# Attention steps ahead of the weight pieces in each turn, and a last slab that makes its two output tiles one behind the other

## The reference, cut to what matters

```python
x = x + _moba(rms(x), w_qkv, w_o)
x = x + conv_ffn(rms(x));  x = rms(x)
x = x + 0.5 * (1 + ga1) * swiglu(mod(rms(x)), w1_gate, w1_up, w1_down)
x = x + (1 + ga2) * hybrid_mixer(mod(rms(x)), w_in, ..., w_o)
x = x + 0.5 * (1 + ga3) * swiglu(mod(rms(x)), w2_gate, w2_up, w2_down)
```

## Time and profile before

| | |
|---|---|
| median of three runs | 819.49 us (819.26 to 819.83) |
| the profiled execution | 819.52 us |
| its span, first to last instruction | 817.3 us, 2.2 us less |
| TensorE busy | 802.3 us (98%) |
| VectorE busy | 644.4 us (79%) |
| ScalarE busy | 487.0 us (60%) |
| HBM read | 177.27 MB, 218 GB/s over the span |

### The profile page before, as it was taken

The page is one execution under the profiler, slowest core; times in us unless marked ns, Lnnn a source line. Parts: engine busy times, 40 slices in busy tenths (PEclk is TensorE's granted clock), DMA queues, the critical chain, the costliest instruction groups (busy, mean ns, idle before and its releaser), DMA issues.

```text
span 817.3 us, 16917 instructions
## 1 busy us (share of the span) xinstructions
PE 802.3 (98%) x6862; PEld 780.7 (96%) x6862; DVE 644.4 (79%) x1333; ACT 487.0 (60%) x1015; POOL 21.2 (3%) x53
## 2 busy tenths in 40 slices
PE   7999999999999999999999999899999999999998
PEld 7999998999999999999999999889889999999998
DVE  5788887888899887999988786977667896775551
ACT  6754566767767565756554556665655775555440
POOL 1000000000000000000000000700000000000000
PEclk9999999999999999999999999999999999999999
DMA  8777673765565998489998887545334578665540
GB/s 290 260 234 226 200 267 128 235 199 188 189 225 166 324 308 286 144 295 336 361 333 292 288 263 222 167 134 175 120 118 156 156 249 274 207 199 194 194 155 27
DMA packets 150013, 179.44 MB, mean 220 GB/s; under 512 B 5680, under 2 KB 139568, under 8 KB 149936
## 3 DMA queue, kind: packets, MB, share of 16 engines
q1 hardware_dynamic: 147680, 177.22, 65.8%
q10 hardware_dynamic: 1232, 1.11, 0.4%
q0 software_dynamic: 1024, 0.03, 0.1%
HBM read 177.27 MB, written 1.05 MB: 218 GB/s over the span
## 4 chain that ended last, share of the span: by engine, by line
PE 77%; DVE 4%; ACT 2%; issue 1%; DVEq 0%; ACTq 0%
PE bank L1349 24%; PE bank L1352 24%; PE bank L1353 24%; DVE wlo L970 1%; PE bank L1451 1%; PE bank L1439 1%; PE bank L1468 0%; PE bank L1370 0%; PE bank L1402 0%; DVE yb L1010 0%; PE bank L1418 0%; DVE A L1021 0%; ACT B L748 0%; PE bank L1395 0%; ACT sq L768 0%
## 5 line engine op out<-in xcount | busy, mean ns | idle before, releaser
L970 DVE TENSOR_TENSOR wlo<-raw,whi 128x512 fp32r<-128x512 f32 x528 | 342.7, 683 | 69.4 <-ACT whi L727 68.7
L727 ACT ACTIVATE whi<-raw 128x512 fp32r<-128x512 f32 x528 | 307.3, 622 | 97.1 <-PE bank L1353 85.2
L1349 PE MATMUL bank<-A,whi 128*128 128x256 f32 x1264 | 357.3, 283 | 3.4 <-DVE wlo L970 2.6
L1352 PE MATMUL bank<-A,whi 128*128 128x256 f32 x1264 | 350.6, 277 | 0.1
L1353 PE MATMUL bank<-A,wlo 128*128 128x256 f32 x1264 | 350.2, 277 | 0.0
L1349 PEld LDWEIGHTS bank<-A,whi 128*128 128x128 f32 x1264 | 237.7, 188 | 6.5 <-DVE wlo L970 3.5
L1352 PEld LDWEIGHTS bank<-A,whi 128*128 128x128 f32 x1264 | 237.7, 188 | 1.2 <-issue 1.0
L1353 PEld LDWEIGHTS bank<-A,wlo 128*128 128x128 f32 x1264 | 237.8, 188 | 0.0
L1349 PE MATMUL bank<-Hhi,whi 128*128 128x256 f32 x528 | 146.2, 277 | 0.0
L1353 PE MATMUL bank<-Hhi,wlo 128*128 128x256 f32 x528 | 145.9, 276 | 0.0
L1352 PE MATMUL bank<-Hlo,whi 128*128 128x256 f32 x528 | 145.9, 276 | 0.0
(11 more groups left out here) (150 smaller groups left out, 811.0 us busy)
## 6 DMA issues: line engine op xcount, KB each, us to landing
mring<-in_w_mod SPq DMA_DIRECT2D x72, 512.0 KB, 6.4
raw<-in_ffn_w_up SPq DMA_DIRECT2D x22, 1024.0 KB, 5.1
raw<-in_w_gate SPq DMA_DIRECT2D x22, 1024.0 KB, 5.7
raw<-in_w_up SPq DMA_DIRECT2D x22, 1024.0 KB, 6.0
raw<-in_w_down SPq DMA_DIRECT2D x16, 1024.0 KB, 5.4
raw<-in_w_in SPq DMA_DIRECT2D x12, 1024.0 KB, 5.4
raw<-in_moba_w_qkv SPq DMA_DIRECT2D x11, 1024.0 KB, 5.5
raw<-in_ffn_w_down SPq DMA_DIRECT2D x8, 1024.0 KB, 6.2
```

The source lines that it names most:

```text
L727: act.activation(whi[:, i % SPL, k0:k1, 0:width], raw[:, i % RAW, k0:k1, 0:width], ACT.Copy).then_inc(s_whi, 1)
L970: dve.tensor_tensor(lo, raw[:, i % RAW, k0:k1, 0:width], hi.bitcast(F32), ALU.subtract).then_inc(s_wlo, 1)
L1349: pe.matmul(o, hi, xh, start=kg == 0 and not (j and halved(g)), stop=False)
L1352: pe.matmul(o, hi, xl, start=False, stop=False)
```

## The change

In the main loop of the plan `attend()` stands ahead of `fill()`. So in each turn the steps of the attention come first in the queues of ScalarE and VectorE, and the hi and lo of later weights behind them. TensorE has no step in `fill`, SP none in `attend`. The transfers keep their order among themselves.

In the last slab TensorE makes tile 6 from all k-tiles as their pieces come, and at the last k-tile the whole of tile 7. A new semaphore, `s_ahead`, says that tile 6 is done; the eviction of tile 6 waits for it alone, that of tile 7 waits for the slab.

```diff
@@ main loop of the plan
                     offer(i + SPL, kt + 1)
+                    attend()
                     if i > 0:
                         fill(pieces(tag, c0, kt))
-                    attend()
@@ VectorE, evict
-                if part == 0 and g not in by_silu:
+                if g == len(groups) - 1:
+                    need.wait_ge(s_ahead, 1)
+                elif part == 0 and g not in by_silu:
                     need.wait_ge(s_chunk, chunk_of_group(g))
...
+                            if n == KD - 1:
+                                need.wait_ge(s_chunk, chunk_of_group(g))
@@ TensorE, multiply
+                if i == len(slabs) - 1:
+                    last_slab(i, kt)
+                    return
...
+            def last_slab(i, kt):
+                ph, tag, c0, k0, nk = slabs[i][:5]
+                g = plan.group_of[i]
+                for j, k in [(0, kt)] + [(1, k) for k in range(nk if kt == nk - 1 else 0)]:
+                    final = k == nk - 1
+                    xh, xl, ncol = here(tag, ph, k0 + k, g)
+                    hi = whi[:, i % SPL, k, j * P:j * P + P]
+                    lo = wlo[:, i % SPL, k, j * P:j * P + P]
+                    o = at(g, j, 0, ncol)
+                    pe.matmul(o, hi, xh, start=False, stop=False)
+                    pe.matmul(o, hi, xl, start=False, stop=False)
+                    ins = pe.matmul(o, lo, xh, start=False, stop=final)
+                    if j == 0 and final:
+                        ins.then_inc(s_ahead, 1)
+                    elif final or (j == 0 and k % 2 == 1):
+                        ins.then_inc(s_chunk, 1)
```

More of the change, by code:

```diff
@@ L503, in build_program @@
         s_xeven, s_xscaled = sem("s_xeven"), sem("s_xscaled")
+        s_ahead = sem("s_ahead")
         s_cond, s_cact, s_msum, s_mod = sem("s_cond"), sem("s_cact"), sem("s_msum"), sem("s_mod")
```

## The result

The changed kernel takes **827.13 us**, the median of 5 runs (825.02 to 830.85), against 819.49 before (5 runs, 819.06 to 819.83). The ratio is 1.0092, 95% interval 1.0076 to 1.0109: slower, by 7.6 us. The forecast was 825.2 us. The runs of the changed kernel lie further apart than those of the kernel before, and in these five the time goes with the mean granted clock of the run: 825.02 and 825.93 at 1.000, 827.13 and 827.49 at 0.998, 830.85 at 0.994. The profiled execution is that last one, the slowest, and this must be kept in mind with all its rows: its span is 828.6 us, 11.3 more than before.

The account below looks back on a forecast made before the run. TensorE, busy for 98% of the span, was taken to bound the kernel. Swap losses of 5.41 us in qkv1 and 0.66 at head 24, less 0.42 at the tail, gave 5.65 us and 825.2 us, range 823.5 to 827.0, wider 821.8 to 828.0.

Parts of the forecast that it names:

- The swap in qkv1: Heads 0, 4 and 8 each lose 1.28 us, head 12 loses 1.57; sum 5.41 us.
- the same lo and eviction come in: At head 0, one lo and one eviction delay scale as at head 4, costing 1.28 us.
- qkv3 and o3: Only steps behind a held lo can lose; `stsum24` at head 24 comes 0.66 us later.
- I take zero for these: Softmax pairs in qkv3 and o3, including head 28's: scale keeps its time, so no cost.
- Weights late: In qkv1 none: lo6.1, the tightest, has 0.98 us left. Rival with late weights: 827.6 to 830.1 us, chance 0.07.
- The tail: Last slab: one addition and one store behind the last matmul instead of two; 0.42 us gained, range 0.3 to 0.8.
- With nothing beside it, a little sooner: Last store, alone at the end, lands slightly faster than as second of two; gain taken as 0.42 instead of 0.40 us.
- Loads: SP's list is unchanged; loads wait no longer than TensorE is late and have a slab's time to spare; no cost.
- The clock: Rival: clock falls to 1.2 GHz for one turn after each of five new waits, adding 6.7 us; 831.9 us, chance 0.01.
- The sum: Whole kernel: 5.41 + 0.66 - 0.42 = 5.65 us slower, forecast 825.2 us.
- the wider range: 821.8 to 828.0 us, reaching down into the absorbed case and up into the late weights.
- rivals: Full gain 817.3 us, chance 0.06; held piece absorbed 821.0, 0.08; weights late 827.6 to 830.1, 0.07; clock 831.9, 0.01.

Follow-up runs that it names:

- e6: Kernel before, with each turn's hi copies ahead of the attention and only the lo steps behind, last slab as before: 822.13 us, ratio 1.0015.
- e7: Kernel before, with one lo step ahead of the attention and the hi copies behind it, last slab as before: 831.08 us, ratio 1.0133.
- e4: Kernel before, with the swap in qkv1 and o1 only, last slab as before: 825.88 us, ratio 1.0071.
- e12_after_again: The changed kernel measured once more with no edit: 826.31 us, ratio 1.0076 to the kernel before.
- e2_tail_only: Kernel before, with the new last slab and its eviction alone, main loop in the old order: 819.99 us, ratio 0.9999.
- e8: Changed kernel, with the three modulation weight loads of o1 moved to up1: 825.26 us, ratio 1.0067 to the kernel before.
- e9: Kernel before, with the three modulation weight loads of o1 moved to up1, as a control: 819.91 us, ratio 0.9998.
- e10: Kernel before, with new last slab, weight pieces ahead only in turns with scores, o1's three modulation loads moved to up1: 817.02 us, ratio 0.9960.
- e1: Kernel before, with the swap alone and the old last slab: 825.80 us, ratio 1.0081.
- e11: Kernel before, with new last slab, weight pieces ahead only in turns with scores or values, attention ahead in others: 816.87 us, ratio 0.9960.

## Why the prediction was right, and where it was not

**The swap in qkv1: right, 5.4 forecast, 5.1 measured.** Taken as the growth of the start-to-start distance in front of the waiting matmul, heads 4 and 8 cost 1.26 and 1.28 us where 1.28 was said, head 12 cost 1.60 where 1.57 was. The traces of e6 and e7 show that it is the held hi and not the lo, e4 that qkv1 is where it happens. Head 0 cost 0.96, not 1.28. The step that failed is "the same lo and eviction come in": they do, but something also goes. ScalarE at head 0, kernel before, then changed:

```profile
25.89 1.66 ACT L727 ACTIVATE whi<-raw 128x512 fp32r<-128x512 f32 x3
27.56 1.28 ACT L705 ACT_TABLE_LOAD   x1
28.86 0.47 ACT L914 ACTIVATE W<-bank,rs 128x256 f32<-128x256 f32 x1
```

```profile
27.12 1.28 ACT L706 ACT_TABLE_LOAD   x1
28.54 0.47 ACT L915 ACTIVATE W<-bank,rs 128x256 f32<-128x256 f32 x1
```

At head 0 alone a table is loaded ahead of the exponentials, and before it stood behind the third hi. With that hi moved, the load starts 0.44 us and the exponentials 0.32 us earlier. There the engine was not idle ahead of the exponentials, so the piece ahead was not free, and moving it gave 0.32 back. Now the load ends at 28.40 and the exponentials wait for the peaks, which end at 28.49, so head 0 has the wait of 1.28 us that heads 4 and 8 have, and not 0.33 and 1.28 on top of each other. The step is the same in all six traces that hold the hi in qkv1 (e7's among them): 0.96 to 0.98.

**qkv3 and o3: right for what was found, 0.66 forecast, 0.67 measured at head 24; but "I take zero for these" was 0.4 us short.** A second `later` costs 0.09 more, a matmul of the mixer at 544 (L1468 before) costs 0.11, and the start of up4 0.16. There four lo steps stand ahead of VectorE's first addition where two stood, and the 0.98 us for which it was idle ahead of that addition cover most of the two that were added: the addition is 11.89 us behind (623.19 before, 635.08 after) where TensorE had been 11.72. I had followed the turns with attention up to the scales, not to the evictions of the group behind them. That TensorE waits 0.99 us for `B` there, 0.50 before, overstates it: in between it had drawn up by 0.3 us through the shorter distances named above, and waits that much longer. In `e12_after_again`, where it hadn't, the same wait is 0.64.

**Weights late: right that none is.** In qkv1 there is no new wait for `wlo` (the row's 1.7 us are the kernel's first microseconds, 2.6 before). lo6.1 ended 0.99 us before TensorE wanted it, 0.98 forecast.

**The tail: right in kind, 0.42 forecast, 0.57 measured.** Of it 0.40 is the second addition. The rest is the store: the last one lands 1.85 or 1.86 us after its issue in the seven traces with the new last slab, and 2.02 to 2.04 in the seven in which it is the second of two. "With nothing beside it, a little sooner" was worth 0.17 where the forecast had put 0.02.

**Loads: wrong.** "A load waits for a lo that is late by no more than TensorE is; a load has a slab's time and more to spare." The last load of o1 is issued 0.8 us later than TensorE's own lateness, since the lo that frees its buffer now starts at 112.80, behind a hi copy that stands behind the exponentials of head 14 (and behind a dot product that ends at the same moment). And it had nothing to spare: ScalarE already waited 2.4 us for it before, and TensorE 0.19 for `acc`. At nearly the same landing time, 7.5 us before and 7.6 in e12, TensorE's wait is 0.19 and 1.07 us: about 0.9 us is the swap's. The rest of the 2.79 goes with the landing in 9.0 us, which the swap need not have caused: `e2_tail_only`, with no swap, has 8.2 us, and waits 0.87. The landing time varies (5.9 to 9.0 us for the same 1 MB in the eleven traces that have the modulation load ahead of it). Without that load it is 5.1, 5.3 and 5.6 us (e8, e9, e10), and the wait is gone.

**The clock: the rival's place wrong, its kind real, its cause open.** None of the five attention waits moved the granted clock of the changed kernel (at `later` too it was 1.00 from 585 to 594), as the earlier trace rows had it for 1.37 us of idle time, there in two pieces of 0.19 and 1.18. But in the profiled execution of the changed kernel it fell to 0.50 in the norm, behind the 2.8 us wait and a second of 1.19, and again at 535.7 for 3.4 us; the lags above put 2.1 and 1.6 us on these. The swap isn't shown as the cause of either. At the norm e4 fell with a wait of 0.49 and e1 and e12 did not with 0.44 and 1.07. At 535 TensorE had waited 1.62 us for an eviction, as it does in the kernel before (1.52) and in e12 (1.52), where the clock stays at 1.00. The Trainium skill, "TensorE: Matmul & The Clock Gate", section "A second HAM failure mode: psum-queue depth-cycling", speaks of short idle times that come frequently between groups of matmuls. The traces don't bear it out for the attention waits 24 us apart; at the norm, which has one wait after another, the clock fell in two of the fourteen profiled executions and stayed up in twelve.

**The sum.** 5.10 + 0.67 + 0.09 + 0.11 + 0.16 - 0.57 = 5.56 us, against 5.65 forecast. That they agree so well is luck: the misses of -0.31 in qkv1, +0.37 in the second block and -0.15 at the end nearly cancel. The median is 827.13, 1.9 us above the forecast and 0.1 above the end of the forecast's own range of 823.5 to 827.0; it lies in the wider range only because that reached up to rivals, and none of those is what happened. The load, which the forecast priced at nothing, and the clock, at one chance in a hundred, account for the excess of the profiled execution (830.85); for the median run, which has no trace but a mean clock of 0.998, this is inferred. The changed kernel once more was at 826.31, e8 at 825.26.

## What to carry to other kernels

In an in-order queue, filler work is free in front of a step that waits for another engine, and behind it costs up to its whole length, less the idle time that follows it (the two lo steps that moved behind the values at the start of up4, some 0.6 us each, cost 0.16). So before an order is changed, read at each step whether its engine idles ahead of it: fill ahead of steps that wait (here the exponentials, 4.08 us of idle time), and put steps whose inputs are already there first. Applied turn by turn this made a loss of 0.8 to 0.9% into a gain of 0.34%. And look where an engine already waits for a load behind some cover: that load has no slack, and shifts elsewhere will show it.

## What the runs showed of the hardware

- The same 1 MB load at the same place of the same queue took 5.9 (e1) to 9.0 us (the changed kernel) from issue to landing in the eleven traces with a 512 KB load issued up to 1.3 us ahead of it, 7.5 in the kernel before; with none issued just ahead of it, it took 5.1, 5.3 and 5.6 us (e8, e9, e10).
- A wait of 1.3 us with TensorE busy before and behind it left the granted clock at 1.00 every time. In the norm of up1 the clock fell to 0.50 in two of fourteen traces: in the changed kernel for 6.8 us, behind waits of 2.79 and 1.19 us, at a cost of 2.1 us, and in e4 for 3.4 us, behind waits of 0.49 and 1.19, at a cost of 1.0. With waits of 0.44 and 1.19 (e1) or 1.07 and 1.19 (e12) it stayed at 1.00. In e7 it was 0.60 over 3 us behind a wait of 1.8 us.
- Of the 61 runs of the kernel before on the three chips of the experiments, those with a mean granted clock of 0.998 took 820.66 to 822.62 us, the two at 0.995 took 823.12 and 822.67, and those at 0.999 and 1.000 took 818.97 to 820.67. So the mean clock does not explain all of the scatter: a run of e12 at 1.000 took 827.66 us, another 825.44. Why a run falls to the lower clock is not settled.
- With the granted clock at 1.00 the same matmuls from 625 to 630 started 0.1178 us apart in the kernel before and in e12, and 0.1133 apart in the changed kernel's profiled execution and in e11. In e9 this difference alone makes 0.94 us between 143 and 175. No run shows what sets it.
- A transpose that waited 0.26 us by the profile cost 0.42 by the starts of the matmuls.
